# More homes for split units in the query's tensor, the first hidden tile of three FFNs turned on VectorE, and the first norm weights fetched inside the first loop

## The reference

```python
for l in range(DEPTH):
    x = layer_norm(ALPHA * x + 0.5 * swiglu(x, ffn1_w13[l], ffn1_w2[l]), ln_g[l, 0], ln_b[l, 0])
    h = x @ w_in[l]
    ...                                   # pool_mixer, mla_mixer with rope(q), rope(k_pe)
    x = layer_norm(ALPHA * x + y_mix, ln_g[l, 1], ln_b[l, 1])
    y_mem = memory_cross_attention(x, mem, mem_wq[l], mem_wkv[l], mem_wo[l])
    x = layer_norm(ALPHA * x + y_mem, ln_g[l, 2], ln_b[l, 2])
    x = layer_norm(ALPHA * x + 0.5 * swiglu(x, ffn2_w13[l], ffn2_w2[l]), ln_g[l, 3], ln_b[l, 3])

def swiglu(x, w13, w2):                   # D_FF = 2816
    gate, up = jnp.split(x @ w13, 2, axis=-1)
    return (jax.nn.silu(gate) * up) @ w2
```

## Time and profile before

| what | us |
|---|---|
| median of 3 runs | 1094.37 |
| profiled execution | 1095.91 |
| its span | 1094.1 |
| TensorE matmul busy | 1082.2 (99%) |
| TensorE weight loads busy | 933.6 (85%) |
| VectorE busy | 847.9 (77%) |
| ScalarE busy | 534.8 (49%) |
| GpSimd busy | 80.4 (7%) |
| mean share of the 16 DMA engines by the weights' queue | 55.1% |

### The profile page before, as it was taken

One profiled execution on the slowest core, in us unless ns is written; L12 is line 12 of the kernel. 1 busy time (PEld: TensorE's weight loads), 2 busy tenths in 40 slices (PEclk: granted clock), 3 DMA queues, 4 the chain that ended last, 5 costly groups with the idle time before them and its releaser, 6 DMA issues.

```text
span 1094.1 us, 16586 instructions
## 1 busy us (share of the span) xinstructions
PE 1082.2 (99%) x5720; PEld 933.6 (85%) x5720; DVE 847.9 (77%) x1450; ACT 534.8 (49%) x731; POOL 80.4 (7%) x120
## 2 busy tenths in 40 slices
PE   9999999999999999999999999999999999999997
PEld 7888887999899888888888888889999988888885
DVE  5888887797866788778687887878977667887885
ACT  5545444566454554444454444445664645444442
POOL 0260000140100100000010000001401000000000
PEclk9999999999999999999999999999999999999999
DMA  8675756354564475665657556554546556556551
GB/s 301 197 213 186 222 184 236 111 161 168 190 214 141 153 233 178 219 189 175 212 184 226 177 182 219 173 196 122 168 152 205 179 170 196 169 192 213 173 189 58
DMA packets 156803, 203.18 MB, mean 186 GB/s; under 512 B 12656, under 2 KB 137840, under 8 KB 156752
## 3 DMA queue, kind: packets, MB, share of 16 engines
q1 hardware_dynamic: 153552, 193.25, 55.1%
q0 software_dynamic: 2912, 8.92, 2.8%
q10 hardware_dynamic: 288, 0.33, 0.1%
HBM read 201.41 MB, written 1.05 MB: 185 GB/s over the span
## 4 chain that ended last, share of the span: by engine, by line
PE 90%; DVE 4%; DMA 2%; issue 2%; SPq 1%; ACT 1%; DVEq 0%; POOL 0%; POOLq 0%; ACTq 0%
PE ps L591 87%; DVE hidden_T L1467 2%; DMA raw<-in_ffn_w 2%; PE ps L674 2%; DVE w_lo L1410 1%; SPq L540 1%; DMA raw<-in_mem_wkv 1%; DVE ev L1453 0%; PE ps L834 0%; DMA cst<-in_constants 0%; ACT ev L1203 0%; DVE tmp L1527 0%; PE ps L1069 0%; DVE x L1516 0%; PE ps L922 0%
## 5 line engine op out<-in xcount | busy, mean ns | idle before, releaser
L1161 ACT CAST w_hi<-raw 128x1024 fp32r<-128x1024 f32 (+1 forms) x247 | 255.7, 1044 | 214.2 <-DMA raw<-in_ffn_w 98.1
L1410 DVE TENSOR_TENSOR w_lo<-raw,w_hi 128x1024 fp32r<-128x1024 f32 (+1 forms) x247 | 295.9, 1222 | 82.7 <-ACT w_hi L1161 80.8
L591 PE MATMUL ps<-w_hi,xT 128*128 128x512 f32 (+1 forms) x912 | 287.3, 389 | 0.5 <-DVE xT L1443 0.5
L591 PEld LDWEIGHTS ps<-w_hi,xT 128*128 128x128 f32 x912 | 171.0, 188 | 35.8 <-DVE xT L1443 0.7
L591 PE MATMUL ps<-w_hi,mixT 128*128 128x512 f32 x688 | 198.1, 390 | 0.1
L1161 ACT CAST v_flat<-raw 128x1024 fp32r<-128x1024 f32 (+1 forms) x114 | 118.7, 1045 | 141.1 <-DMA raw<-in_ffn_w 77.8
L1467 DVE STREAM_TRANSPOSE hidden_T<-ev 32x128 f32<-32x128 f32 x576 | 174.5, 303 | 8.6
L591 PE MATMUL ps<-v_flat,xT 128*128 128x512 f32 (+1 forms) x660 | 177.2, 389 | 0.0
L591 PE MATMUL ps<-w_lo,xT 128*128 128x512 f32 (+1 forms) x456 | 175.3, 388 | 0.0
L591 PEld LDWEIGHTS ps<-w_hi,mixT 128*128 128x128 f32 x688 | 128.7, 188 | 26.8 <-issue 0.5
L591 PEld LDWEIGHTS ps<-v_flat,xT 128*128 128x128 f32 x660 | 123.7, 188 | 25.3 <-DVE cqp L1410 0.2
(11 more groups left out here) (168 smaller groups left out, 1223.2 us busy)
## 6 DMA issues: line engine op xcount, KB each, us to landing
raw<-in_ffn_w SPq DMA_DIRECT2D x352, 256.0 KB, 3.7
raw<-in_ffn_w SPq DMA_DIRECT2D x88, 512.0 KB, 5.2
raw<-in_mem_wkv SPq DMA_DIRECT2D x32, 512.0 KB, 4.8
raw<-in_w_out SPq DMA_DIRECT2D x16, 512.0 KB, 4.6
raw<-in_mem_wq SPq DMA_DIRECT2D x16, 512.0 KB, 5.8
raw<-in_mem_wo SPq DMA_DIRECT2D x16, 512.0 KB, 4.6
gb<-in_ln_g POOLq DMA_DIRECT2D x8, 512.0 KB, 4.4
gb<-in_ln_b POOLq DMA_DIRECT2D x8, 512.0 KB, 6.2
```

What stands on the lines that cost most here:

```text
L591: return nc.tensor.matmul(dst, stand, move, start=start, stop=stop, skip_group_check=True)
L1161: nc.scalar.copy(slot_hi[slot[n]][:, 0:size], raw[:, n % RAW, 0:size]).then_inc(hi_done, 1)
L1410: nc.vector.tensor_tensor(slot_lo[slot[n]][:, s], raw[:, n % RAW, s], slot_hi[slot[n]][:, s].bitcast(F32), ALU.subtract).then_inc(lo_done, 1)
```

## The change

1. **Homes in `qT`.** `qT`, the query's tensor, holds two more slots (numbers 10 and 11), usable for the units from the first `mem_wkv` unit behind FFN 0 and FFN 4 up to the unit `kn`. In layer 1 the first two must wait for a mark of layer 0.
2. **Step 0 turned by blocks** in the FFNs 3, 4 and 7: `by_blocks(e, s)` is true for step 0 unless e is 0. The 4 transposes on TensorE go; 16 STREAM_TRANSPOSEs come on VectorE right behind `multiply(0)`, and `down(0)` waits for `hidden_lo`.
3. **Angles in `poolM`** rather than in `gb`, so that the first `load_gains` waits for nothing. Positions, that load and the angles now start when TensorE has finished unit 23 of the first FFN instead of unit 11; the wait for `tables_done` goes to the first `RMS` of layer 0.

```diff
-    BLOCK_TURNED = FS - 2
+    BLOCK_TURNED = FS - 1
@@ plan_ffn
-            marks += [UNIT_] * 2 + ([[("hidden", e, 0)]] if s == 1 else []) + (turned(2) + turned(3) if e == 0 and s == 1 else [])
+            marks += [UNIT_] * 2 + ([[("hidden", e, 0)]] if e == 0 and s == 1 else []) + (turned(2) + turned(3) if e == 0 and s == 1 else [])
@@ slots
-    latest = [k - SLOTS for k in range(SLOTS)] + [-1] * 4
+    latest = [k - SLOTS for k in range(SLOTS)] + [-1] * 6
+    QUERY_HOMES = [SLOTS + 4, SLOTS + 5]
...
+            if plan["kv", *FILL[l, "ln0"][0]]["units"] <= n <= plan["kn", l]["units"]:
+                usable += QUERY_HOMES
+                if l and n < plan["kv", *FILL[l, "ln0"][0]]["units"] + 2:
+                    after = done["mscore", l - 1, 1]
...
-        for spent in (memT, memK):
+        for spent in (memT, memK, qT):
@@
-        def by_blocks(s):
-            return 0 < s < FS - 1
+        def by_blocks(e, s):
+            return e + s > 0 and s < FS - 1
@@ tensor, up
-                        if j == 1 and s == 1:
+                        if j == 1 and s == 1 and e == 0:
                             turn_hidden(0)
@@ scalar and vector, ffn
-                ahead_to(u + 7) if e == 0 else ahead(("hidden", e, 0))
+                ahead_to(u + 7) if e == 0 else ahead(("unit", u + 5))
@@ gpsimd
-            pool.wait_ge(pe_done, done["unit", plan["ffn", 0, 0]["units"] + 11])
+            pool.wait_ge(pe_done, done["unit", plan["ffn", 0, 0]["units"] + 23])
             for b in range(TB):
-                pool.dma_start(gb[:, 1, b:b + 1].bitcast(I32),
+                pool.dma_start(pool_flat[:, place:place + 1].bitcast(I32),
...
+            load_gains(0)
             rope_angles()
...
-            pool.wait_ge(tables_done, 1)
-            load_gains(0)
             for l in range(L):
                 norm(4 * l)
+                if l == 0:
+                    pool.wait_ge(tables_done, 1)
```

More of the change, by code:

```diff
@@ L478, in trunk @@
         poolB = tiles(gb[:, 1, 0:512], 2)
+        pool_flat = poolM[:, :, :].rearrange("p t s -> p (t s)")
         def by_head(t):
@@ L726, in ffn @@
             def ffn(l, w):
-                e, f, turns = 4 * l + 3 * w, (2 * l + w) * FS, 2 * (2 * l + w)
+                e, f = 4 * l + 3 * w, (2 * l + w) * FS
                 blocks = (2 * l + w) * BLOCK_TURNED
@@ L829, in turn_hidden @@
                 def turn_hidden(s):
-                    pe.wait_ge(rows_ready, turns + (1 if s == 0 else 2))
+                    pe.wait_ge(rows_ready, 1 if s == 0 else 2 * l + w + 2)
                     for b in range(TB):
@@ L842, in wait_hidden @@
                 def wait_hidden(s, it=None):
-                    if by_blocks(s):
+                    if by_blocks(e, s):
                         pe.wait_ge(hidden_lo, plus(blocks + s, it, STEPS))
@@ L1472, in split_hidden @@
                     dve.wait_ge(columns_hi, plus(f + s + 1, it, STEPS))
-                    last = nc.vector.tensor_tensor(hidden_columns(s, 1), hidden_source(s, m),
+                    last = nc.vector.tensor_tensor(hidden_columns(s, 1), hidden_source(e, s, m),
                                                    hidden_columns(s, 0).bitcast(F32), ALU.subtract)
-                    if by_blocks(s):
+                    if by_blocks(e, s):
                         last.then_inc(hidden_lo, 1)
@@ L1806, in rope_angles @@
                 n = TB * HALF
-                ang, turns, part_of = gb[:, 0, 2 * n:3 * n], gb[:, 0, 3 * n:4 * n], gb[:, 0, 4 * n:5 * n]
-                own(nc.gpsimd.tensor_copy(gb[:, 1, TB:2 * TB], gb[:, 1, 0:TB].bitcast(I32)))
+                ang, turns, part_of = (pool_flat[:, k * n:(k + 1) * n] for k in (2, 3, 4))
+                places = pool_flat[:, 5 * n:5 * n + 2 * TB]
+                own(nc.gpsimd.tensor_copy(places[:, TB:2 * TB], places[:, 0:TB].bitcast(I32)))
                 for b in range(TB):
                     own(nc.gpsimd.tensor_scalar(ang[:, b * HALF:(b + 1) * HALF], cst[:, C_FREQ:C_FREQ + HALF],
-                                                gb[:, 1, TB + b:TB + b + 1], None, ALU.mult))
+                                                places[:, TB + b:TB + b + 1], None, ALU.mult))
                 for i, quarter in enumerate((0.25, 0.0)):
-                    r = gb[:, 0, i * n:(i + 1) * n]
+                    r = pool_flat[:, i * n:(i + 1) * n]
                     own(nc.gpsimd.tensor_scalar(turns, ang, 1.0 / (2.0 * math.pi), quarter, ALU.mult, ALU.add))
@@ L1845, in _ @@
             clear_keys()
-            pool.wait_ge(pe_done, done["unit", plan["ffn", 0, 0]["units"] + 11])
+            pool.wait_ge(pe_done, done["unit", plan["ffn", 0, 0]["units"] + 23])
             for b in range(TB):
-                pool.dma_start(gb[:, 1, b:b + 1].bitcast(I32),
+                place = 5 * TB * HALF + b
+                pool.dma_start(pool_flat[:, place:place + 1].bitcast(I32),
                                a["positions"][0, b * P:(b + 1) * P].rearrange("(p o) -> p o", o=1)).then_inc(pos_landed, 16)
+            load_gains(0)
             rope_angles()
```

8 lines of the change are left out of this document (4 added, 4 removed).

## The result

The changed kernel takes 1107.94 us (median of 5 runs, 1105.28 to 1109.70) against 1094.37, a ratio of 1.0123 with the 95% interval [1.0112, 1.0134]: 13.6 us slower. The forecast was 1100.4, and the range ended at 1103.5. The direction was right and the size too small by more than half. The profiled execution of the changed kernel took 1109.70 us (span 1107.9), 1.8 above its median.

A forecast was written before the change was run, and what follows sets the result against it. TensorE's own work, busy 99% of the span, was taken as the bound. Terms -1.3 + 2.0 + 4.2 + 1.1 = +6.0 us on the 1094.37 us median gave 1100.4 us; 8-in-10 range 1096.2 to 1103.5.

The forecast's parts named there:

- Norm weights: First loop, `down(4)` of FFN 0: one weight load 2.3 us late, less 1.2 us of slack, +1.1 us.
- Homes: Ends of FFNs 0 and 4: units ahead of the last product make TensorE wait 2.4 and 1.8 us more, +4.2 us.
- First steps: FFNs 3, 4, 7: transposes gone, -1.3 us; `down(0)` waits 1.0, 1.0 and 0 us, +2.0.
- forecast wait of 3.7 us: `turn_hidden(10)` at the end of FFN 0: TensorE waits 3.7 us for the product.
- The signs: `turn_hidden(10)` of FFNs 0, 4 waits 3.7, 1.8 us; `down(0)` of FFNs 3, 4 and `down(4)` of FFN 0 about 1.
- Faster: Rival: first `w_in` unit lands by 180.0 and 728.6, waits at FFN ends go, -3.4 us, 1091.0; chance 0.06.
- The delay carries on: Rival: loops of FFNs 3, 4, 7 stay late, norm weights cost the full 2.3 us, +11.1, 1105.5; chance 0.14.
- the homes give nothing back: Later `w_in` splits come sooner, but TensorE waited for none, and layer 1's 0.8 us wait stays: no gain.

The follow-up runs named there:

- Run 5: The kernel before, unchanged, profiled a second time: 1094.12 us, one run.
- Run 1: The kernel before with only the two homes in the query's tensor `qT`: 1100.02 us, ratio 1.0051.
- Run 2: The kernel before with only the angles in the other tensor, and positions, first norm weights and angles moved behind unit 23: 1098.99 us, ratio 1.0040.
- Run 10: The kernel before with angles and positions moved behind unit 23, but only `ln_g` fetched there and `ln_b` behind the sine tables: 1097.10 us, ratio 1.0024.
- Run 9: The kernel before with only angles, positions and first norm weights moved, behind unit 21 of the first FFN instead of 23: 1094.58 us, ratio 1.0002.
- Run 13: The kernel before with the two homes, but splits at the ends of FFNs 0 and 4 limited to where they stood before: 1095.28 us, ratio 1.0009.
- Run 3: The kernel before with only step 0 of FFNs 3, 4 and 7 turned by blocks on VectorE: 1095.60 us, ratio 1.0011.
- Run 4: The changed kernel with the first norm weights fetched behind the sine tables as before: 1100.70 us, ratio 1.0056.
- Run 8: The kernel before with nine idle ScalarE copies ahead of the last silu of FFN 0, making TensorE wait: 1101.06 us, ratio 1.0055.
- Run 11: The kernel before with step 0 turned by blocks in FFN 7 alone: 1094.17 us, ratio 0.9999.
- Run 7: The changed kernel with no next-stage unit split ahead of `gate(10)` and `multiply(10)` in FFNs 0 and 4: 1106.66 us, ratio 1.0113.

## Why the prediction was wrong in size

The direction and the places were right; two things failed. The term of the norm weights was mis-sized, 1.1 us where 4.6 were measured. And what the parts do to each other was put at nothing without a reason, where 2.1 us were measured, mostly with a fall of TensorE's clock. Of the 7.5 us that the forecast was short, these two make 5.6; the homes make 1.4 and the first steps 0.5.

The starts of equal matmuls, the changed kernel against Run 5, give the account by place (the executions took 1109.70 and 1094.12 us, so it is the account of an execution 1.8 us above the median):

| behind | later by | this step |
|---|---|---|
| `down(1)` of FFN 0 | 0.5 | 0.5 |
| the first loop | 5.3 | 4.7 |
| the wait at `turn_hidden(10)`, FFN 0 | 9.8 | 4.5 |
| the stretch at half clock | 12.2 | 2.5 |
| `down(0)` of FFN 3 | 12.9 | 0.7 |
| `down(0)` of FFN 4 | 13.4 | 0.5 |
| `turn_hidden(10)` of FFN 4 | 15.2 | 1.8 |
| mixer of layer 1 | 15.8 | 0.6 |
| FFN 7 | 15.5 | -0.3 |

The first 0.5 also stands in Run 1, which has no part of the change before that place, and not in Run 2; it belongs to the execution.

**Norm weights, +1.1 forecast, +4.6 measured (Run 2).** The mechanism and the place (`down(4)`) were right, the term was mis-sized. I took the difference of two single loads, 6.8 - 4.5 = 2.3 us, once, and took a slack of 1.2 off it. The slack held (Run 10); the delay at `gate(4)` was 4.6 us instead of 2.3. The two transfers were issued into a burst in which loads queue behind each other, and the whole burst finishes later by the time of the bytes added: two transfers of 512 KB at the 270 GB/s that the DMA engines moved in this window of Run 2 are an estimated 3.9 us. The delay less the slack is 3.4 us, and so late was TensorE at `down(4)`, after the waits at `up(5)` and there; 0.9 more came at `down(5)` and 0.5 at `turn_hidden(10)`, which I had not counted. The Trainium skill (DMA: Bandwidth & Descriptors, Queues, rings and completion order) says that each DMA engine takes turns between the queues that have work for it; the rows agree, since GpSimd's two transfers and SyncE's loads all landed late together (5.9 and 8.2 us against 4.5 and 5.8 in Run 9, and 7.3 against 4.1). Runs 9 and 10 show that it is the meeting that costs.

**Homes, +4.2 forecast, +5.6 [4.0, 7.0] measured (Run 1).** The mechanism was right: two more units ahead of the last product. In Run 1 the first unit of `w_in` was issued at 175.93 and landed 6.0 us later, and TensorE turned at 184.73, 2.8 us behind it; the forecast had 176.35, 6.0 and 2.75. Run 13 shows that little but this order costs. Two things were off. The prediction subtracted the start at 182.72 in the earlier trace rows, which had a wait of 1.27 us in it that Run 5 hasn't: a wait that comes and goes with the execution was taken for a property of the kernel. It explains most of the 1.5 us by which that execution lay above the median, and it hid 1.3 us of the cost. And the 0.6 us in layer 1's mixer was set at nothing, though the order there had changed.

**First steps, +0.7 forecast, +1.2 [0.2, 2.2] measured (Run 3).** Right, by place too: the transposes gave 0.44 us for a forecast of 0.45, and in the changed kernel `mixT` was waited for 0.89 and 0.64 us in FFNs 3 and 4 against 1.0 and 1.0, and not in FFN 7.

**What the parts do together, nothing forecast, 2.1 us measured.** Runs 1, 2 and 3 sum to 11.5 us (before rounding), and the change cost 13.6. Their intervals reach 1.0 to 1.5 us to each side, so the medians alone don't prove the difference; the traces do. The late loop still ran late at its end (`gate(9)` 2.34 us behind `up(9)`, against 0.78 in Run 5). So the first `w_in` unit was issued at 182.13, and the wait at `turn_hidden(10)` was 4.36 us instead of the 3.37 of Run 4; and with this longer wait the clock fell, 2.5 us. Run 8 shows the fall with a long wait alone. The five executions of the changed kernel fit: four took 1107.94 to 1109.70 us with a mean granted clock of 0.995 or 0.996, and one took 1105.28 with 0.998, a value that the kernel before also has. That one lies 10.9 us above the kernel before, close to the sum of the parts. There is no trace of it, so that the clock stayed up in it is read from the mean alone. The prediction summed waits as if TensorE came out of them as fast as it went in. The Trainium skill (TensorE: Matmul & The Clock Gate, Why this matters for your kernels) warns of idle gaps of TensorE between matmul bursts, behind which it runs at half rate. The rows agree for the waits of 4.36 and 4.05 us, and not for those of 3.37 and 2.83 us, behind which the granted clock was still 1.0. The prediction cited that page for a transpose and never held its own forecast wait of 3.7 us against it. By the runs it would have been right to make it a rival.

**The signs.** The changed kernel has nearly all that the prediction named: waits of 4.36 and 1.60 us at the two ends (3.7 and 1.8 forecast), 0.89 and 0.64 for `mixT`, 1.07 at `down(4)`. What it didn't name, the waits at `up(5)` and `down(5)` and the stretch at half clock, makes 5.8 of the 15.5 us.

**The rivals.** "Faster" needed the first `w_in` unit by 180.0; it landed at 188.1. "The delay carries on" fell: in FFN 3 `gate` began 3.46 us behind the start of `down(0)` at step 1 and 0.20 behind that of `down(7)` by step 8, with no wait of TensorE between. In the first loop the norm weights did cost more than the full 2.3 us of that rival. That the homes give nothing back was right: the 0.3 us in FFN 7 are the transposes', since Runs 3 and 11 have them without homes.

## What to carry to other kernels

Before a transfer is moved into a loop, look at the DMA share of that stretch in small windows: the same 1 MB cost 4.6 us on top of a burst and nothing 4.8 us sooner. A buffer more is also permission for a look-ahead rule to put more work in front of what is urgent; give the buffer and the limit together. And profile the kernel before twice: a wait that one execution has and the next hasn't hides part of the cost of whatever makes that place later.

## What the runs showed of the hardware

**The clock.** TensorE's granted clock fell from 1.0 to 0.50 in waits of 4.36 us (the changed kernel) and 4.05 us (Run 8), was back some 7 us later, and cost 2.5 us each time; after 3.37 us (Run 4) and 2.83 us (Run 1) it had stayed at 1.0. The wait's length alone doesn't decide it: in Run 7 it fell within 1 us behind a wait of 1.92 us, and cost 1.5 us, and did not behind one of 1.87 us at the same place of layer 0. Behind both waits TensorE makes eight small transposes and then 24 matmuls of 256 columns. What tells these two apart stays open. In a profile such a stretch shows as longer instructions and higher busy time, in no wait: the profiled executions with a fall have 1084.7 to 1085.3 us of busy time of TensorE (the changed kernel, Runs 7 and 8), all others 1081.5 to 1083.2.

**Transfers beside a burst.** With two transfers of 512 KB beside them, the 256 KB loads of the burst took 7.3 us instead of 4.1 and the 512 KB loads 8.0 instead of 5.8 (Run 2), while the DMA engines' share was 0.97 to 1.01 from 79 to 85 us.
